# Twenty-one block products instead of ten in a feed-forward projection, with ScalarE and GpSimd sharing the work beside them

## What is computed

```python
def conv_ffn(h, w_up, conv_w, conv_b, w_down):
    u = causal_dwconv(h @ w_up, conv_w, conv_b)      # w_up: 1024 x 5632, three taps along the tokens
    val, gt = jnp.split(u, 2, axis=-1)               # 2816 value channels, 2816 gate channels
    return (jax.nn.silu(gt) * val) @ w_down
```

```python
mod   = jax.nn.silu(c) @ w_mod[li] + b_mod[li]       # w_mod: 1024 x 6144
mod_c = jax.nn.silu(c_ctx) @ w_mod[li] + b_mod[li]   # only its first 2048 columns are used
```

## Time and profile before

| | |
|---|---|
| three runs | 3170.92, 3176.77, 3177.23 us; median 3176.77 |
| the profiled execution | 3176.86 us |
| its span in the trace | 3174.8 us |
| TensorE busy | 2985.4 us, 94% |
| VectorE, ScalarE, GpSimd busy | 1531.8, 578.7, 868.8 us |
| the stage of the change | 1506.5 to 1796.4 us of the span |

### The profile page before, as it was taken

How to read it: one execution, slowest core, us unless ns; L and a number is a source line. 1 busy time by engine, 2 the same in 40 slices (tenths; PEclk the granted TensorE clock), 3 DMA queues, 4 the chain that set the end, 5 groups by cost and what they waited for, 6 DMA issues and landing times. The chain is left out here.

```text
span 3174.8 us, 52013 instructions
## 1 busy us (share of the span) xinstructions
PE 2985.4 (94%) x22044; PEld 2067.1 (65%) x22044; DVE 1531.8 (48%) x2497; ACT 578.7 (18%) x1074; POOL 868.8 (27%) x592
## 2 busy tenths in 40 slices
PE   9999999999999789999999998999879997999998
PEld 6855857986887678667666685368768853443433
DVE  5764756336555466534877663663534323011112
ACT  2142040012001333111000002111443312100101
POOL 1111222101121545211999880011355310000000
PEclk9999999999999899999999999999999998999999
DMA  4242223221321000132334442122200016999996
GB/s 163 90 165 79 80 82 111 80 80 36 124 80 47 3 4 4 48 127 80 132 127 152 144 159 75 63 86 68 69 12 3 22 52 264 378 409 409 409 409 273
DMA packets 122228, 412.62 MB, mean 130 GB/s; under 512 B 13568, under 2 KB 21376, under 8 KB 121744
## 3 DMA queue, kind: packets, MB, share of 16 engines
q1 hardware_dynamic: 112784, 373.64, 32.5%
q0 software_dynamic: 9216, 35.66, 3.3%
HBM read 404.97 MB, written 4.28 MB: 129 GB/s over the span
## 5 line engine op out<-in xcount | busy, mean ns | idle before, releaser
L942 PE MATMUL ps<-arena 128*128 128x256 f32 x4536 | 994.3, 381 | 15.4 <-PEq L900 6.8
L942 PEld LDWEIGHTS ps<-arena 128*128 128x128 f32 x4536 | 857.9, 191 | 159.7 <-issue 35.5
L998 PE MATMUL ps<-arena 128*128 128x512 f32 (+1 forms) x880 | 350.8, 557 | 10.4 <-DVE arena L1322 7.3
L998 PEld LDWEIGHTS ps<-arena 128*128 128x128 f32 x880 | 169.2, 194 | 184.4 <-issue 173.7
L880 POOL TENSOR_TENSOR arena<-arena 128x512 f32<-128x512 f32 x64 | 90.0, 1407 | 609.6 <-DMA arena<-in_w_in 258.0
L3788 PE MATMUL ps<-arena 128*64 128x512 f32 x1024 | 224.6, 594 | 9.3 <-DMA arena<-in_w_up 6.9
L886 POOL TENSOR_TENSOR arena<-arena 128x512 f32<-128x512 f32 x64 | 81.3, 1270 | 454.5 <-PE ps L942 454.5
L1227 DVE TENSOR_TENSOR arena<-ps,arena 128x256 f32<-128x256 f32 x81 | 34.4, 425 | 339.2 <-PE ps L942 338.2
L1159 DVE SCALAR_TENSOR_TENSOR arena<-ps,params,arena 128x511 f32<-128x511 f32 (+4 forms) x266 | 190.7, 717 | 9.4
L3929 POOL TENSOR_SCALAR arena<-arena,small 128x1024 f32<-128x1024 f32 x64 | 191.4, 2990 | 10.7 <-DMA arena<-in_w_mod 7.0
L3788 PEld LDWEIGHTS ps<-arena 128*64 128x64 f32 x1024 | 83.9, 137 | 148.6 <-issue 148.4
(11 more groups left out here) (440 smaller groups left out, 4038.1 us busy)
## 6 DMA issues: line engine op xcount, KB each, us to landing
arena<-in_w_in SPq DMA_DIRECT2D x166, 512.0 KB, 3.6
arena<-in_w_gate SPq DMA_DIRECT2D x128, 512.0 KB, 15.3
arena<-in_w_up SPq DMA_DIRECT2D x128, 512.0 KB, 15.2
arena<-in_w_down SPq DMA_DIRECT2D x128, 512.0 KB, 15.3
arena<-in_w_mod POOLq DMA_DIRECT2D x48, 512.0 KB, 4.2
arena<-in_ffn_up SPq DMA_DIRECT2D x44, 512.0 KB, 3.7
arena<-in_w_branch SPq DMA_DIRECT2D x32, 512.0 KB, 3.7
arena<-spill POOLq DMA_DIRECT2D x16, 640.0 KB, 5.4
```

What stands on the lines that cost most here:

```text
L942: last = nc.tensor.matmul(k.bank(b)[:, 0:HT], lhs[:, q * P:(q + 1) * P], rhs[:, q, :], start=(first and q == 0), stop=(q == 3), skip_group ...
L998: last = nc.tensor.matmul(out[0:j["m"], 0:j["n"]], w[:, q * m:(q + 1) * m], j["rhs"](q), start=(n == 0), stop=(n == kn - 1))
```

## The change

All but the first two upward planes become pairs (2 plain units and 21 pairs), and `pool` goes back to its default, so that GpSimd makes S1 and S3. With `tap_by_act` the first tap with its bias is made by ScalarE from PSUM (`first_tap`); VectorE waits for it and adds the other two. Two planes are used in turn for the value planes before their product, and a semaphore (`multiplied`) tells ScalarE when one is free again. `ModSide` takes the place of `mod_products` in this stage: ScalarE scales a modulation tile (in place, or into one of two spare pairs of planes for the second condition), GpSimd only adds and issues the loads. ScalarE does its share of an index n inside the unit of planes 2n and 2n+1, GpSimd its share n behind the weight sums of pair n.

```diff
@@ fast_phase, GpSimd
                 for u in splits[opening:]:
                     sum_op(pool, nc.gpsimd, u, "S1", k.st_sump)
                     sum_op(pool, nc.gpsimd, u, "S3", k.st_sump)
+                    if between is not None:
+                        between(pool, u["s"])
@@ fast_phase, ScalarE
+            def first_tap(u, m):
+                j = jobs[u["i"] + m]
+                if not j.get("tap_by_act"):
+                    return
+                if u["kind"] == "S":
+                    act.wait_ge(*put_together(u, "C12" if m == 0 else "C21"))
+                    src = raw(u, m)
+                else:
+                    act.wait_ge(k.piece_done, piece0 + u["i"] + 1)
+                    src = k.bank(u["bank"][0])[0:j["m"], 0:j["n"]]
+                if j.get("mul_n", 0) > 2:
+                    act.wait_ge(k.multiplied, j["mul_n"] - 2)
+                nc.scalar.activation(j["dst"], src, ACT.Identity, bias=j["bias"], scale=j["taps"][0][0]).then_inc(k.tapped, 1)
...
                 if u["kind"] == "S":
                     late = u
                 else:
+                    first_tap(u, 0)
                     finish(u, 0)
                 if side is not None:
                     for n in range(len(js)):
                         side.act(act, u["i"] + n)
+                if u["kind"] == "S":
+                    first_tap(u, 0)
+                    first_tap(u, 1)
@@ fast_phase, VectorE, finish
-                    if j.get("bias") is not None:
+                    if j.get("tap_by_act"):
+                        dve.wait_ge(k.tapped, j["tap_n"])
+                        ins = None
+                    elif j.get("bias") is not None:
@@
+                        if j.get("mul_n"):
+                            nc.vector.engine_nop().then_inc(k.multiplied, 1)
@@ new
+class ModSide:
+    def __init__(self, k, acc, parts, turned, units):
+        self.steps = [(t, q) for t in parts for q in range(KT)]
+        self.work = [(m, who) for m, (t, q) in enumerate(self.steps) for who in ((1, 0) if t < 2 else (0,))]
+        self.part = lambda n: self.work[len(self.work) * n // units:len(self.work) * (n + 1) // units]
...
+    def act(self, act, i):
+        k = self.k
+        if i % 2 == 1 or i // 2 >= self.units:
+            return
+        if i == 0:
+            act.wait_ge(k.c_ok, 2)
+        for m, who in self.part(i // 2):
+            n = self.work.index((m, who))
+            act.wait_ge(self.mod_in[m % 2], 16 * (m // 2 + 1))
+            if who and m >= 2:
+                act.wait_ge(self.added, self.work.index((m - 2, 1)) + 1)
+            k.nc.scalar.activation(self.product(m, who), self.weight(m), ACT.Copy, scale=...).then_inc(self.scaled, 1)
+
+    def between(self, pool, s):
+        k = self.k
+        if s == 0:
+            self.load(pool, 0)
+            self.load(pool, 1)
+        for m, who in self.part(s):
+            n = self.work.index((m, who))
+            pool.wait_ge(self.scaled, n + 1)
+            if self.steps[m][1]:
+                pool.wait_ge(self.added, n)
+                k.nc.gpsimd.tensor_tensor(self.sum(m, who), self.sum(m, who), self.product(m, who), ALU.add).then_inc(self.added, 1)
+            else:
+                k.nc.gpsimd.engine_nop().then_inc(self.added, 1)
+            if who == 0 and m + 2 < len(self.steps):
+                pool.wait_ge(self.added, n + 1)
+                self.load(pool, m + 2)
@@ program
-        up = Halves(k, [u for i in range(0, 40, 4) for u in (("C", i), ("C", i + 1), ("S", i + 2, 0))] + [("C", i) for i in range(40, 44)], [dict(x=H_PL, t=WORK + 8)], [MRG_PL + 4 + n for n in range(4)] + [WORK + 59], [WORK + 60],
-                    pool=False)
-        plan(k, project_phase, k, js, beside=mod_products(k, acc, range(0, 4), 2), ahead=ffn_norm, halves=up)
+        up = Halves(k, [("C", 0), ("C", 1)] + [("S", i, 0) for i in range(2, 44, 2)], [dict(x=H_PL, t=WORK + 8)],
+                    [MRG_PL + 4 + n for n in range(4)] + [WORK + 59], [WORK + 60])
+        mods = ModSide(k, acc, range(0, 4), [acc + 16, WORK + 16], 20)
+        plan(k, project_phase, k, js, ahead=ffn_norm, halves=up, side=mods, between=mods.between)
```

More of the change, by code:

```diff
@@ L335, in wtile, with project_phase @@
     return [(w[i, :, a * P:min(a + 8, kt) * P], a, min(8, kt - a)) for a in range(0, kt, 8)]
[L338 removed]
+def project_phase(k, jobs, following=(), beside=None, moves=(), ahead=None, side=None, halves=None, afterwards=None, tail=None, loads=None, between=None):
     if halves is not None:
[L347 removed]
+        return fast_phase(k, jobs, halves, following, beside, moves, ahead, afterwards, tail, side, between)
     nc = k.nc
@@ L803, in fast_phase @@
         ahead.begin()
+    shared = [j for j in jobs if j.get("tap_by_act")]
+    if shared:
+        k.tapped, k.multiplied = (k.sem(f"{x}{k.nc.next_id()}") for x in ("tapped", "multiplied"))
+        for n, j in enumerate(shared):
+            j["tap_n"] = n + 1
+        for n, j in enumerate(j for j in shared if j.get("mul") is not None):
+            j["mul_n"] = n + 1
     mul0, cop0, sumd0, sump0, asm0, t0 = k.n_mul, k.n_cop, k.n_sumd, k.n_sump, k.n_asm, k.n_t
@@ L1156, in finish @@
                     for c, sh in j["taps"][1:]:
-                        link(ins)
+                        if ins is not None:
+                            link(ins)
                         o, s = (dst[:, sh:n], src[:, 0:n - sh]) if sh > 0 else (dst[:, 0:n + sh], src[:, -sh:n])
@@ L3933, in mod_products, with begin, weight, sum @@
     return gpsimd
+class ModSide:
+    def __init__(self, k, acc, parts, turned, units):
+        self.k, self.acc, self.units = k, acc, units
+        self.steps = [(t, q) for t in parts for q in range(KT)]
+        self.work = [(m, who) for m, (t, q) in enumerate(self.steps) for who in ((1, 0) if t < 2 else (0,))]
+        self.turned = turned
+        self.part = lambda n: self.work[len(self.work) * n // units:len(self.work) * (n + 1) // units]
+    def begin(self, jobs, moved, n):
+        self.mod_in = [self.k.sem(f"mod_in_a{i}") for i in range(2)]
+        self.scaled, self.added = self.k.sem("mod_scaled"), self.k.sem("mod_added")
+    def weight(self, m):
+        return self.k.pl(MRG_PL + 2 * (m % 2), 2)
+    def sum(self, m, who):
+        return self.k.pl(self.acc + 12 * who + 2 * self.steps[m][0], 2)
+    def product(self, m, who):
+        if self.steps[m][1] == 0:
+            return self.sum(m, who)
+        return self.k.pl(self.turned[m % 2], 2) if who else self.weight(m)
+    def load(self, pool, m):
+        t, q = self.steps[m]
+        pool.dma_start(self.weight(m), self.k.dram["w_mod"][q * P:(q + 1) * P, t * 1024:(t + 1) * 1024]).then_inc(self.mod_in[m % 2], 16)
+    def pe(self, pe, i):
+        pass
+    def dve(self, dve, i):
+        pass
+    def act(self, act, i):
[9 more added lines that the diff above has]
+                act.wait_ge(self.added, self.work.index((m - 2, 1)) + 1)
+            k.nc.scalar.activation(self.product(m, who), self.weight(m), ACT.Copy, scale=k.small[:, 2 * self.steps[m][1] + who:2 * self.steps[m][1] + who + 1]).then_inc(self.scaled, 1)
+    def between(self, pool, s):
[14 more added lines that the diff above has]
+                self.load(pool, m + 2)
@@ L4081, in order @@
                 js.append(job(wtile(dr["ffn_up"], FT + i), H, "D", pl(hid + i), taps=t(FT + i),
-                              bias=k.col("ffn_conv_b", FT + i), post=silu))
+                              bias=k.col("ffn_conv_b", FT + i), post=silu, tap_by_act=True))
             for i in (c, c + 1):
-                js.append(job(wtile(dr["ffn_up"], i), H, "D", pl(tmp), taps=t(i), bias=k.col("ffn_conv_b", i),
-                              mul=pl(hid + i), needs=len(js) - 2))
-        up = Halves(k, [u for i in range(0, 40, 4) for u in (("C", i), ("C", i + 1), ("S", i + 2, 0))] + [("C", i) for i in range(40, 44)], [dict(x=H_PL, t=WORK + 8)], [MRG_PL + 4 + n for n in range(4)] + [WORK + 59], [WORK + 60],
-                    pool=False)
-        plan(k, project_phase, k, js, beside=mod_products(k, acc, range(0, 4), 2), ahead=ffn_norm, halves=up)
+                js.append(job(wtile(dr["ffn_up"], i), H, "D", pl((tmp, WORK + 61)[i % 2]), taps=t(i), bias=k.col("ffn_conv_b", i),
+                              mul=pl(hid + i), needs=len(js) - 2, tap_by_act=True))
+        up = Halves(k, [("C", 0), ("C", 1)] + [("S", i, 0) for i in range(2, 44, 2)], [dict(x=H_PL, t=WORK + 8)],
+                    [MRG_PL + 4 + n for n in range(4)] + [WORK + 59], [WORK + 60])
+        mods = ModSide(k, acc, range(0, 4), [acc + 16, WORK + 16], 20)
+        plan(k, project_phase, k, js, ahead=ffn_norm, halves=up, side=mods, between=mods.between)
         last_norm = Norm(k, lambda c: pl(X + c), lambda c: pl(X + c), lambda c: k.col("norm_final", c), WORK + 8, early=True, squares=2)
```

4 lines of the change are left out of this document (1 added, 3 removed).

## The result

| | before | changed |
|---|---|---|
| median of the runs taken side by side (6 each) | 3175.12 us | 3185.86 us (3181.71 to 3191.34) |
| ratio, with its 95% interval | | 1.0033 [1.0023, 1.0042] |
| span of the profiled execution | 3174.8 us | 3179.6 us |
| stage, first plain plane to the first product of the downward part | 289.7 us | 299.3 us |

The changed kernel is slower by 0.33%; I had forecast 3171.4 us and a range from 3160 to 3181. The code ahead of the stage is the same in every kernel here, yet the stage begins between 1498.3 and 1511.4 us in their profiled executions. So stages are compared by their own length, and kernels by medians. A stage's length is that of one execution, whose whole time can lie several us from the median of its kernel (3181.71 against 3185.86 here, 3185.40 against 3176.25 in run 1).

A forecast was written before the change was run, and what follows sets the result against it. The prediction took PE to bound the stage. From 3176.86 us, -18.0 (pairs) + 0.5 (VectorE's chain) + 9.9 (loads) + 2.1 (seam) gave 3171.4 us, with a range of 3160 to 3181.

The forecast's parts named there:

- PE, eleven pairs more: Upward stage: eleven more pairs at 12.09 us instead of 13.73 for two plain planes, -18.0 us if PE never stops.
- DVE's chain and the shared port: VectorE's work in value pairs fits under PE, except two pairs where the last product meets GpSimd's S1: +0.5 us.
- ACT held by loads: Pairs 13, 16, 18: ScalarE's third scaling waits for a late load and holds the taps, so PE waits: +9.9 us.
- the seam: End of the stage, where all engines meet: PE's pause grows from 3.93 to 6.0 us, +2.1.
- the head: Start of the stage: costs nothing, PE's first two planes covering the turns and the taps.
- My timetable: Predicted start and end times of each engine's work within a pair, counted from the pair's first product P1.
- The landings: Time from a modulation tile's load issue until it is there: 4.7 us, with ends 3.6 and 7.3.
- The clock: Rival: PE's clock falls in the pauses of three pairs; 3179.8 us for all three, 3174 for one; chance 0.1.
- The third rival: Slower by the shared port: second products meet a whole GpSimd add, 1.6 us in ten value pairs, 3187; chance 0.15.
- The first rival: ScalarE's scalings do not hold the taps, so no stalls on loads: 3161.5 us; chance 0.25.

The follow-up runs named there:

- run 1: The changed kernel with three slots for modulation tiles instead of two, nothing else: 3176.25 us, 0.9998 of the kernel before.
- run 2: The changed kernel with three slots for modulation tiles and GpSimd's 42 modulation adds left out: 3164.02 us, 0.9961 of the kernel before.
- run 6: The changed kernel with three slots and a gap behind each of GpSimd's weight sums S1 and S3: 3167.52 us, 0.9973 of the kernel before.
- run 3: The changed kernel, two slots, with GpSimd's first weight sums held until the normalized input is ready: 3185.74 us, 1.0032 of the kernel before.
- run 4: Only the pairs of the change; VectorE makes all weight sums and taps, GpSimd the modulation as before: 3187.99 us, 1.0036 of the kernel before.

## Why the prediction was wrong, by its own steps

The terms against the changed kernel's stage (289.7 before, 284.2 forecast, 299.3 measured):

| step | forecast | measured |
|---|---|---|
| PE, eleven pairs more | -18.0 | holds: 12.09 a pair (run 2) |
| DVE's chain and the shared port | +0.5 | 0.58 + 0.18 + 4.27 = 5.0 of pause, 2.9 of half clock |
| ACT held by loads | +9.9 | 3.84 + 0.63, 1.79, 5.53 = 11.8, and 2.1 of half clock (80 records in 19.54, worth 17.3 + 0.16) |
| the seam | +2.1 | 5.94 - 3.76 = 2.2 |
| the head | 0 | +1.7 of half clock; 0.9 of pause, ahead of the stage |

These make +7.7; the measured +9.6 is 1.9 more. It lies in the rows of PE: each of the eight groups that a pause ends is 0.15 to 0.6 us longer, clock apart, than its records at 12.09 per 56 (61.02 for 280, worth 60.45), 2.1 in all, against 0.2 for the one before.

**The step that failed** is "Where GpSimd has three adds, the last product meets S1 (1.27): 0.2 to 0.3 late, in two pairs; +0.5 us". The meeting took place where I put it, but I charged one GpSimd instruction where VectorE waits for all that follow without a gap: 5.51 us for the product, not 2. With what followed, the step cost 7.9 us (5.0 of pause, 2.9 of half clock), not 0.5. My timetable also had S1 end just before P6 of the next pair was done, which would have left a gap; it ended 0.5 us behind. Without the 0.93 us that an add had waited for ScalarE it would have ended before (my reading of the rows, no run tests it). My row for the price, an add of VectorE that ends 0.55 behind GpSimd's, comes from a stage in which each of GpSimd's instructions waited for the one before it, so that there was a gap (0.10 us behind the add in that row); S1, S3 and the first add have none. And what came before and after that add was a scaling, under which VectorE could work:

```profile
1658.31 2.85 POOL L3929 TENSOR_SCALAR arena<-arena,small 128x1024 f32<-128x1024 f32 x1
1659.91 0.68 DVE L886 TENSOR_TENSOR arena<-arena 128x512 f32<-128x512 f32 x1
1660.51 0.68 DVE L892 TENSOR_TENSOR arena<-arena 128x512 f32<-128x512 f32 x1
...
1663.68 3.16 POOL L3929 TENSOR_SCALAR arena<-arena,small 128x1024 f32<-128x1024 f32 x1
```

The Trainium skill (SBUF — State Buffer, section SBUF: two separate sides) says that the pair belongs to one side for one whole instruction; the lengths in runs 1, 2 and 6 agree for two-input adds, and add that the next GpSimd instruction takes it again if it is ready. The scaling in these rows, under which two sums of VectorE took 0.68 us each, does not agree with it, and the measurement decides.

**The loads** were right in mechanism and place, and the three sizes near (3.2, 2.0, 4.7 against 4.5, 1.8, 5.5). The landings were the mis-sized part: 4.7 in my sum, 6.5 and 7.3 measured, the 7.3 being the end that I had kept for the range; the 3.85 in pair 16 gave something back. With these landings my timetable gives 5.0, 1.2 and 7.3, 13.5 in all against 11.8, so the landings are more than the whole excess. Run 1 prices the step at 9.6 us of time, net of the new pause in pair 15.

**The head** "costs nothing", I wrote, and put no term for it. I had not asked what GpSimd's new first sums meet there: S3 holds up VectorE's first product of the norm (run 3), 0.9 us of pause. The 1.7 us of half clock behind it I count as chance, as under run 3.

**The clock** I had as a rival with one chance in ten, for pauses at the loads. It fell at pair 9 and pair 18, not at 13 with 3.84 us of pause. Two of the three large pauses took it along, for 5.0 us together; the sum should have carried a part of that price.

**The third rival** (slower, the shared port) named the right engine and the right sign, but as a steady 1.6 us in ten value pairs. It was one pair with all of it. **The first rival** would have been 3161.5; run 2 shows 3164.0 with its conditions met (and the adds gone); the head, with 2.6 us in its profiled execution, is as large as the rest. Right too: 1.14 us for a scaling (1.16), the seam's 6.0 (5.94), GpSimd at 58% of the stage. A tap took 0.78, not 0.69.

So where did the gain go? 18 us came; about 14 went to loads that were issued behind GpSimd's adds, 8 mostly to one lost turn, 4 to head and seam. With a third slot and two gaps the same change is 0.3% faster than before, not 0.3% slower.

## What to carry to other kernels

If one engine's result is wanted soon, do not put an instruction that waits for a load in front of it on the same queue; one more slot was worth about 10 us here. If GpSimd works beside VectorE, price a meeting by GpSimd's whole run up to its next wait, not by one instruction, and give it a gap (a signal to itself) where VectorE is on PE's path. With the third slot the gaps brought 8.7 us; with two slots they took the pause away, and a gain in time was not resolved. And price a pause of PE with the half clock that may follow it, here 2.1 and 2.9 us.

## What the runs showed of the hardware that I had not expected

- A VectorE product of two SBUF tiles (0.69 us alone) took 5.51 us across three two-input GpSimd instructions that followed each other without a gap, and 2.01 us with a gap of 0.1 us behind the first. Under a GpSimd scaling of one tile (2.85 us) VectorE's sums took 0.68 us.
- It works the other way round too: the GpSimd instruction behind the gap then took 1.59 us instead of 1.28.
- The clock fell behind a pause of 4.27 us and not behind one of 3.84 us in the same run; in run 4 it fell behind 2.06 us and not behind 2.63; at the head the same two planes ran at full or half clock behind either length of pause. The length of the pause alone does not decide it.
- Three tiles of the same size were there 3.85, 6.5 and 7.3 us after their issue, within one stage.
